# Mean squares from the input rows and convolution taps on sixteen 32 by 32 tiles, in a streaming encoder step

## The chip, the core and the metric

The kernel runs on one core of a Trainium2 chip. The metric is the device time of one execution in microseconds. The kernel before was run three times: 1377.0, 1381.54 and 1380.49 us, median 1380.49.

## The reference, cut to what matters

Two layers over 544 tokens (512 prompt frames and 32 frames of a running stream) with 1024 channels. Layer 0 is attention beside a gated linear recurrence, layer 1 a convolution module; each is followed by a squared-ReLU MLP. The change touches the first normalisation and the depthwise convolution:

```python
def rms_norm(x, g):
    xf = x.astype(jnp.float32)
    y = xf * lax.rsqrt(jnp.mean(xf * xf, axis=-1, keepdims=True) + EPS)
    return (y * g.astype(jnp.float32)).astype(x.dtype)

def conv_module(xn, buf, w1, b1, w_dw, b_dw, ln_g, ln_b, w2, b2):
    u = xn @ w1 + b1
    u = u[..., :D_MODEL] * jax.nn.sigmoid(u[..., D_MODEL:])
    full = jnp.concatenate([buf.astype(u.dtype), u], axis=1)
    y = lax.conv_general_dilated(full, w_dw.astype(full.dtype)[:, None, :], window_strides=(1,),
                                 padding='VALID', dimension_numbers=('NWC', 'WIO', 'NWC'),
                                 feature_group_count=D_MODEL) + b_dw
    y = jax.nn.silu(layer_norm(y, ln_g, ln_b))
    return y @ w2 + b2, full[:, -(CONV_W - 1):]
```

The depthwise convolution has 31 taps per channel (`CONV_W` = 31), and it is causal: the prompt is preceded by 30 zeros, the running stream by 30 cached rows.

## The kernel before

**Layout.** Activations lie with channels on the 128 partitions and tokens along the free dimension: `resid` is 8 channel tiles (`KT`) of 544 tokens. Each projection streams weights in units of 256 output columns (two halves m of 128). SP loads a unit to `w_raw`, ACT copies it to `w_h` as fp32r (`split_hi`, L585), DVE subtracts to get `w_l` (`split_lo`, L1456), and TensorE (PE) sums three products, w_h by x_h, w_h by x_l and w_l by x_h, each in two column halves of 272: 96 fp32r matmuls per unit (L983, or L1006 where both halves m advance together). Two double-bank slots of PSUM hold the two halves m. Semaphores order everything: `w_lo` counts split units, `gemm_done` finished halves, `slot_free` evacuated slots, `xl_ready` finished input tiles.

**Prologue.** SP loads the input rows (`x_rows`, L365, L366), then weight unit 0, then 19 small parameter transfers (L368 to L385), then weight unit 1. PE transposes the rows into channel tiles through the two slots (L944). DVE copies each tile to `resid` (L1511); ACT multiplies by the norm's gain into `x_h` (L615) and squares the tile (L606); POOL adds the squares (L460); DVE makes `x_l` (L1478). The split of unit 0 stands within these loops: at k = 3 on ACT, at k = 5 on DVE. PE transposes the parameters before unit 0 (L947 to L957) and takes the mean of the squares by a matmul with `mean_d` between the two halves of unit 0 (`mean_square`, L1041, L968). ACT takes the root (L621), DVE the reciprocal over 544 columns (L1484), and the result `r_tok` scales every evacuation of the first projection (L1548).

**Convolution stage.** Unit m of the first pointwise projection gives the two halves of channel tile m. ACT takes the sigmoid (L853); DVE makes the gated frames `glu` (`gated_frames`, L1849). The 31 taps of a tile are split: PE does 14 (16 in the last tile, m = 7) and DVE 17 (15). On PE a tap is a matmul with a diagonal matrix. The array is used as four tiles of 64 by 64: the diagonal is `fold` (two halves of the identity added) scaled by the tap's weights (ACT, L862), a tap t takes `glu` straight, its partner t + 7 takes `glu_swap`, a copy with the two halves of the partitions exchanged that POOL's queue makes by two transfers per tile (L557). `add_taps` (L1353) issues, for each of 7 pairs and 2 column halves of 288, four matmuls in plain fp32, 56 per tile; each fp32 matmul appears as two MATMUL records in the trace, 112 per tile. The columns cover prompt, gap and running stream in one row of 576 (`CW`). DVE runs its 17 taps over the same 576 columns on two accumulators (`conv_taps`, L1871, L1875, L1878) with the next unit's `split_lo` after the eighth, then adds the four PSUM parts in two instructions and the two accumulators in one (`conv_sum`, L1888, L1890). PE's order is: `gated(m+1)`, then the taps of m, and so on; after the last, matmuls with `mean_d` (L1363) take the channel mean for LayerNorm, with the taps of tile 7 after the third of them. `keep_clock` (L959) issues bf16 matmuls into an unused bank, only to keep PE active.

The lines that set the order around the change:

```python
            pairs = tap_pairs(m)
            pe.wait_ge(conv_ready, m + 1)
            x = glu[:, m, :]
            for pair in pairs:
                for c in range(2):
                    for across in range(2):
                        for r in range(2):
```

Of the kernel before, what the change touches and what calls it, by code (L numbers as in the profile page):

```python
# [41 lines left out]
PE_TAPS = 14  # L42
PAIRS = PE_TAPS // 2
LAST_PAIR = (PE_TAPS, PE_TAPS + 1)
CROSS = LAST_PAIR[1] + 1 - PAIRS
# [39 lines left out]
def hybrid_kernel(nc, x_prompt, x_sample, cache_a_k, cache_a_v, state_b, cache_c, norm_mix_g, norm_ffn_g,  # L85
# [35 lines left out]
    dw_swap = sb(ctx, "dw_swap", [P, KT, CROSS])  # L121
# [9 lines left out]
    no_use = sb(ctx, "no_use", [P, 1])  # L131

# [15 lines left out]
    with ExitStack() as over:  # L148
        sb(over, "under_x", [P, 2, KT, TOK])
        with ExitStack() as mix:  # L150
            x_rows = sb(mix, "x_rows", [P, TT + 1, D])
            dw_rows = sb(mix, "dw_rows", [CONV, D])
            dw_cross = sb(mix, "dw_cross", [CROSS, D])
            cc_rows = sb(mix, "cc_rows", [PAD, D])

# [20 lines left out]
        with ExitStack() as mix:  # L176
# [6 lines left out]
            glu_swap = sb(mix, "glu_swap", [P, 2, FW])  # L183
            diag = sb(mix, "diag", [P, 2, PE_TAPS + 2, P // 2])
            fold = sb(mix, "fold", [P, P // 2])
# [45 lines left out]
    def width(c):  # L231
# [8 lines left out]
    consts = sem("consts")  # L240
    gains_T, gains_ready = sem("gains_T"), sem("gains_ready")
    r_ready = sem("r_ready")
# [31 lines left out]
    glu_edges, conv_step, conv_ready, cvmean, cv_centred, cv_sq, cv_var, cv_std, cv_norm, cv_silu = (  # L274
        sem(n) for n in ("glu_edges", "conv_step", "conv_ready", "cvmean", "cv_centred", "cv_sq",
                         "cv_var", "cv_std", "cv_norm", "cv_silu"))
    cv_hi, cv_lo, swapped = sem("cv_hi"), sem("cv_lo"), [sem("swapped0"), sem("swapped1")]
# [58 lines left out]
    def tap_pairs(m):  # L336

        return [(t, t + PAIRS) for t in range(PAIRS)] + ([LAST_PAIR] if isinstance(m, int) and m == KT - 1 else [])

# [22 lines left out]
    def _(sp):  # L362
# [5 lines left out]
        def load_parameters():  # L368
# [9 lines left out]
            for h in range(2):  # L378
                to, of = (a.rearrange("t (k h c) -> t k h c", h=2, c=P // 2) for a in (
                    dw_cross[:], c_w_dw[0, PAIRS:PAIRS + CROSS]))  # L380
                sp.dma_start(to[:, :, h, :], of[:, :, 1 - h, :]).then_inc(rows_landed, 16)
# [49 lines left out]
    def _(pool):  # L431
# [8 lines left out]
        pool.memset(ones[:], 1.0)  # L440
        pool.memset(mean_d[:], 1.0 / D)
        pool.memset(eps[:], EPS)
# [27 lines left out]
        for k in range(KT):  # L470
            sum_squares(0, k, k % 2, k == 0)

# [12 lines left out]

        pool.wait_ge(xl_ready, KT)
# [62 lines left out]
        pool.tensor_tensor(fold[:], ident[:, 0:P // 2], ident[:, P // 2:P], ALU.add).then_inc(glu_edges, 1)  # L549

        for m in range(KT):
# [3 lines left out]
            for b in range(2):  # L555
                to, of = slice(b * (P // 2), (b + 1) * (P // 2)), slice((1 - b) * (P // 2), (2 - b) * (P // 2))
                pool.dma_start(glu_swap[to, m % 2, :], glu[of, m, :]).then_inc(swapped[m % 2], 16)  # L557
# [9 lines left out]
    def _(act):  # L567
# [33 lines left out]
        def square(n, k, parity, ready, at):  # L601

            act.wait_ge(ready, at)
            if not (n == 0 and isinstance(k, int) and k < 2):
                act.wait_ge(sumsq_step, k + (8 * n - 1))
# [17 lines left out]
        act.wait_ge(consts, 1)  # L623
# [7 lines left out]
        act.wait_ge(vec_ready, 1)  # L631
        act.activation(wlr_h[:, :, 0:RANK], wlr[:], ACT.Copy).then_inc(wlr_hi, 1)
# [34 lines left out]
        for u in range(U_ATT):  # L667
# [4 lines left out]
            if u == 0:  # L672
                frame_std(0)
# [3 lines left out]
            if u < 4:  # L677
                square_qk(u, 0)
                square_qk(u, 1)
        copy_rows(6)  # L680
# [175 lines left out]
        def diagonals(i, s):  # L856
# [3 lines left out]
            for pair in tap_pairs(m):  # L860
                for t, w, at in ((pair[0], w_dw, m * CONV + pair[0]), (pair[1], dw_swap, m * CROSS + (pair[1] - PAIRS))):
                    ins = act.activation(diag[:, s, t, :], fold[:], ACT.Identity,  # L862
# [1136 lines left out]
```

## Time and profile before

| | |
|---|---|
| median of the three runs | 1380.49 us |
| time of the profiled execution | 1379.77 us |
| its span, first to last instruction | 1378.0 us |
| PE, DVE, ACT, POOL busy | 1348.9, 722.5, 466.7, 82.1 us |
| convolution stage: `gated(1)` to the last mean matmul | 767.7 to 918.6 us of the span |

Busy shares are averages over stages with different limits; for a change in one stage, the chain of waits and the timeline of that stage are the views to read. Matmuls are pipelined: the duration of one record includes filling and draining, and the distance between starts is what it costs.

### The profile page before, as it was taken

How to read it: one execution, taken by the hardware profiler on the slowest of the kernel's cores; microseconds unless marked ns; L12 is line 12 of the kernel's file. 1: busy time of each engine (PE TensorE's matmuls, PEld its weight loads, DVE VectorE, ACT ScalarE, POOL GpSimd, SP SyncE). 2: the span in 40 equal slices, each digit the busy share in tenths (PEclk: the TensorE clock that was granted, in tenths of full speed). 3: DMA queues.
4: the chain of work that ended last, by engine and by line, in shares of the span. 5: the costliest groups of instructions: out<-in, count | busy, mean ns of one | idle time of the engine just before them, and what ended most of it. 6: DMA issues, size and time to landing. Idle time of an engine off the chain costs nothing.

```text
span 1378.0 us, 26679 instructions
## 1 busy us (share of the span) xinstructions
PE 1348.9 (98%) x11208; PEld 1279.1 (93%) x11208; DVE 722.5 (52%) x1034; ACT 466.7 (34%) x743; POOL 82.1 (6%) x116
## 2 busy tenths in 40 slices
PE   6999999999999999999999999999999999999998
PEld 5999788789999999999999888868999999999998
DVE  6684568675543334334324799897544333324322
ACT  4221556534333213223122433336333213213121
POOL 5100100001100000000011000001100000000000
PEclk9999999999999999999999999999999999999999
DMA  5422410122222222222221222112222322222221
GB/s 172 158 76 86 150 32 1 70 97 85 69 92 92 92 92 92 92 74 79 96 88 62 75 77 80 52 39 69 93 92 79 97 77 85 92 92 92 92 78 49
DMA packets 105590, 115.62 MB, mean 84 GB/s; under 512 B 3761, under 2 KB 102684, under 8 KB 105245
## 3 DMA queue, kind: packets, MB, share of 16 engines
q1 hardware_dynamic: 102621, 101.47, 22.9%
q0 software_dynamic: 2816, 12.84, 2.9%
q8 instruction: 69, 1.13, 0.3%
q14 instruction: 20, 0.16, 0.0%
q10 hardware_dynamic: 64, 0.02, 0.0%
HBM read 104.62 MB, written 7.21 MB: 81 GB/s over the span
## 4 chain that ended last, share of the span: by engine, by line
PE 90%; DVE 5%; ACT 3%; issue 1%; DMA 0%; POOL 0%; SPq 0%; ACTq 0%; DVEq 0%; POOLq 0%
PE ps L983 70%; PE ps L1353 4%; PE ps L1116 4%; PE ps L1006 2%; DVE rstd L1552 2%; PE ps L1133 1%; PE ps L964 1%; PE ps L1227 1%; PE ps L1166 1%; PE ps L1150 1%; PE ps L1022 1%; DVE w_l L1456 1%; PE ps L968 1%; ACT w_h L585 1%; PE ps L1363 1%
## 5 line engine op out<-in xcount | busy, mean ns | idle before, releaser
L585 ACT ACTIVATE w_h<-w_raw 128x2048 fp32r<-128x2048 f32 x92 | 175.3, 1905 | 274.0 <-PE ps L983 270.9
L1456 DVE TENSOR_TENSOR w_l<-w_raw,w_h 128x2048 fp32r<-128x2048 f32 x92 | 211.7, 2301 | 104.5 <-ACT w_h L585 104.4
L983 PE MATMUL ps<-x_h,w_h 128*128 128x272 f32 x1184 | 247.6, 291 | 2.6 <-ACT sig L853 1.5
L983 PE MATMUL ps<-x_l,w_h 128*128 128x272 f32 x1184 | 245.6, 289 | 0.0
L983 PE MATMUL ps<-x_h,w_l 128*128 128x272 f32 x1184 | 245.3, 289 | 0.0
L983 PE MATMUL ps<-xf_l,w_h 128*128 128x272 f32 x1024 | 211.0, 288 | 0.0
L983 PE MATMUL ps<-xf_h,w_h 128*128 128x272 f32 x1024 | 211.0, 288 | 0.0
L983 PE MATMUL ps<-xf_h,w_l 128*128 128x272 f32 x1024 | 210.5, 287 | 0.0
L983 PEld LDWEIGHTS ps<-x_h,w_h 128*128 128x128 f32 x1184 | 187.2, 190 | 6.8 <-issue 6.3
L983 PEld LDWEIGHTS ps<-x_h,w_l 128*128 128x128 f32 x1184 | 187.4, 190 | 0.0
L983 PEld LDWEIGHTS ps<-x_l,w_h 128*128 128x128 f32 x1184 | 186.5, 189 | 0.0
L983 PEld LDWEIGHTS ps<-xf_h,w_l 128*128 128x128 f32 x1024 | 160.7, 188 | 0.0
L983 PEld LDWEIGHTS ps<-xf_h,w_h 128*128 128x128 f32 x1024 | 160.4, 188 | 0.2
L983 PEld LDWEIGHTS ps<-xf_l,w_h 128*128 128x128 f32 x1024 | 160.1, 188 | 0.0
L1796 DVE TENSOR_TENSOR resid<-ps,resid 128x544 f32 x64 | 46.3, 723 | 198.2 <-PE ps L983 197.2
L829 ACT ACTIVATE relu<-relu 128x544 f32<-128x544 f32 x64 | 42.2, 659 | 237.7 <-DVE relu L1814 237.7
L983 PE MATMUL ps<-odd_h,w_h 128*128 128x272 f32 x512 | 106.0, 288 | 0.0
L983 PE MATMUL ps<-odd_l,w_h 128*128 128x272 f32 x512 | 105.6, 288 | 0.0
L983 PE MATMUL ps<-odd_h,w_l 128*128 128x272 f32 x512 | 105.4, 287 | 0.0
L1814 DVE SCALAR_TENSOR_TENSOR relu<-ps,xn 128x544 f32<-128x544 f32 x64 | 46.2, 722 | 87.4 <-PE ps L983 87.3
L983 PEld LDWEIGHTS ps<-odd_h,w_l 128*128 128x128 f32 x512 | 80.3, 188 | 0.0
L983 PEld LDWEIGHTS ps<-odd_h,w_h 128*128 128x128 f32 x512 | 80.1, 189 | 0.1
(258 smaller groups left out, 1682.6 us busy)
## 6 DMA issues: line engine op xcount, KB each, us to landing
w_raw<-in_w_ffn_up SPq DMA_DIRECT2D x32, 1024.0 KB, 5.4
w_raw<-in_w_ffn_down SPq DMA_DIRECT2D x32, 1024.0 KB, 5.1
w_raw<-in_w_in_ab SPq DMA_DIRECT2D x12, 1024.0 KB, 5.2
w_raw<-in_c_w_pw SPq DMA_DIRECT2D x12, 1024.0 KB, 5.8
w_raw<-in_w_out_ab SPq DMA_DIRECT2D x4, 1024.0 KB, 5.3
glu_swap<-glu POOLq DMA_DIRECT2D x16, 151.5 KB, 2.5
resid_scratch<-resid POOLq DMA_DIRECT2D x1, 2176.0 KB, 7.5
resid<-resid_scratch POOLq DMA_DIRECT2D x1, 2176.0 KB, 8.9
```

Of the source, the lines that this page charges most:

```text
L585: act.activation(w_h[s][:], w_raw[:, s], ACT.Copy).then_inc(w_hi, 1)
L829: act.activation(relu2[:, m, :], relu[:, m, :], ACT.Square).then_inc(relu2_done, 1)
L964: pe.matmul(ps[:, bank, 0:2 * P], any_bits[:, 0:P], any_bits, start=True, stop=True)
L968: ins = pe.matmul(dst[:, a, :], w[:], src[:, a * n:(a + 1) * n], start=start, stop=stop)
L983: ins = pe.matmul(ps[:, 2 * m + t, 0:HALF], a[s][:, k, w], b[:, k, t * HALF:(t + 1) * HALF], start=(k == 0 and q == 0), stop=(k == KT - 1 ...
L1006: ins = pe.matmul(ps[:, 2 * m + t, 0:HALF], a[s][:, k, w], b[:, k, t * HALF:(t + 1) * HALF], start=(k == 0 and q == 0), stop=(k == KT - 1 ...
L1116: ins = pe.matmul(ps[:, 2 * m + t, 0:HALF], a[u % 2][:, k, m * P:(m + 1) * P], b[:, k, t * HALF:(t + 1) * HALF], start=(k == 0 and q == 0) ...
L1353: ins = pe.matmul(sum_ps(r, CH)[to, c, :], diag[rows, s, tap, :], src, start=(pair is pairs[0]), stop=(pair is pairs[-1]))
L1456: dve.tensor_tensor(w_l[s][:], w_raw[:, s], w_h[s][:].bitcast(F32), ALU.subtract).then_inc(w_lo, 1)
L1552: dve.reciprocal(rstd[:, 0:TOK], sumsq[:]).then_inc(rstd_ready, 1)
L1796: dve.tensor_tensor(r, slot(m), r, ALU.add).then_inc(slot_free[m], 1)
L1814: dve.scalar_tensor_tensor(out=halves(relu[:, m, :]), in0=slot(m), scalar=0.0, in1=halves(r_tok), op0=ALU.max, op1=ALU.mult).then_inc(slot ...
```

## The change

**Prologue.** The mean squares come from the input rows, where tokens are partitions: DVE squares and sums rows 0 to 2 (`tensor_tensor_reduce`), ACT rows 3 and 4 (`Square` with `accum_out`), then root and reciprocal run on a 128 by 5 tile, POOL widens it (`r_wide`), and PE transposes it within unit 0 into the slot that is not in use. The transposes of x use four slots of two banks; ACT copies tiles 6 and 7 in place of DVE. DVE does all its copies first, then the split of unit 0, then the `x_l`. Unit 0 runs both halves m together. The parameters are loaded after both first weight units (23 transfers in place of 19) and transposed after unit 0. PE issues 16 bf16 matmuls at the start and 24 between the first transposes.

**Convolution.** `ROTS` = 4, `SET` = 6: tap j*6 + n takes a copy of `glu` rotated by 32*j partitions; 5 rounds n (6 in tile 7) of 4 rotations and 4 row groups: 80 matmuls of 512 columns on 32 by 32 tiles per channel tile (96 in the last). DVE has 11 taps (7 in the last) over 512 columns; the running stream's 32 frames are computed by DVE as one product over all windows and one reduction. Six transfers per tile instead of two, 20 diagonals (24) of 32 columns instead of 14, four PSUM additions instead of two. On DVE the sum of tile m-1 now comes after the gated frames of m, and the split after the taps.

```diff
-PE_TAPS = 14
+ROTS = 4
+SET = 6
+PE_TAPS = ROTS * SET
@@ SP
             if first:
                 for s in range(2):
                     sp.dma_start(w_raw[:, s], source(s)).then_inc(w_landed[s], 16)
-                    if s == 0:
-                        load_parameters()
+                load_parameters()
@@ POOL
-        for k in range(KT):
-            sum_squares(0, k, k % 2, k == 0)
...
+        pool.wait_ge(r_rows, 1)
+        pool.tensor_copy(r_wide[:], x_rs[:].unsqueeze(2).to_broadcast((P, TT + 1, P))).then_inc(r_spread, 1)
...
+            for j in range(1, ROTS):
+                at = P - j * (P // ROTS)
+                pool.dma_start(glu_rot[0:at, m % 2, j - 1, :], glu[P - at:P, m, 0:PAD + SEQ]).then_inc(moved[m % 2], 16)
+                pool.dma_start(glu_rot[at:P, m % 2, j - 1, :], glu[0:P - at, m, 0:PAD + SEQ]).then_inc(moved[m % 2], 16)
@@ ACT
+        act.activation(no_use[:], eps[:], ACT.Sqrt)
         act.wait_ge(gains_ready, 1)
         for k in range(KT):
-            hi_gain(0, x_h, k, V_MIX, slot_free[k % 2], k // 2 + 1)
-            if k == 3:
+            hi_gain(0, x_h, k, V_MIX, x_copied[k % 4], k // 4 + 1)
+            if k == 1:
                 split_hi(0, 0, 0)
-            square(0, k, k % 2, slot_free[k % 2], k // 2 + 1)
+                for late in (6, 7):
+                    act.wait_ge(gemm_done, late + 1)
+                    act.activation(resid[:, late, :], flat(late % 4)[:, 0:TOK], ACT.Copy).then_inc(x_copied[late % 4], 1)
...
+        act.activation(x_rs[:], x_ss[:], ACT.Sqrt, bias=eps[:, 0:1], scale=1.0 / D).then_inc(std_ready, 1)
@@ PE
+        pe.wait_ge(ones_ready, 1)
+        keep_clock(16, 6)
...
+                    keep_clock((0, 14, 6, 2, 2)[c], 6)
...
+        def x_ready(k):
+            if k == KT - 2:
+                pe.wait_ge(r_spread, 1)
+                for c in range(TT + 1):
+                    M = width(c)
+                    ins = pe.transpose(flat(2)[:, c * P:c * P + M], r_wide[0:M, c, :], ident[0:M, 0:M])
+                ins.then_inc(r_T, 1)
+            pe.wait_ge(xl_ready, X_MIX0 + k + 1)
...
+        together(0, 0, x_h, x_l, x_ready)
+        parameters()
...
+        def taps(m):
+            s = m % 2
+            pe.wait_ge(diag_ready, m + 1)
+            pe.wait_ge(slot_free[1], m + (tile0(U_PW1) // 2 + 1))
+            pe.wait_ge(moved[s], (m // 2 + 1) * 96)
+            if m:
+                pe.wait_ge(conv_step, m * STEPS)
+            for n in range(rounds(m)):
+                for j in range(ROTS):
+                    for r in range(ROTS):
+                        rows, to = (slice(h * (P // ROTS), (h + 1) * (P // ROTS)) for h in (r, (r + j) % ROTS))
+                        tap = j * SET + n
+                        src = glu_rot[rows, s, j - 1, tap:tap + SEQ] if j else glu[rows, m, tap:tap + SEQ]
+                        ins = pe.matmul(ps[to, 4 + r, :], diag[rows, s, tap, :], src, start=(n == 0),
+                                        stop=(n == rounds(m) - 1))
+            ins.then_inc(taps_done, 1)
...
+        for m in range(1, KT):
+            gated(m)
+            taps(m - 1)
         pe.wait_ge(slot_free[0], tile0(U_PW2) // 2)
-        for k in range(3):
+        for k in range(4):
             add_mean(k)
-        add_taps(KT // 2 - 1, 1)
+        taps(KT - 1)
@@ DVE
+        for c in range(3):
+            dve.wait_ge(x_landed[c], 16)
+            if c:
+                dve.wait_ge(x_sums, c)
+            dve.tensor_tensor_reduce(sq[:].rearrange("p a t -> p (a t)")[:, 0:D], x_rows[:, c, :], x_rows[:, c, :], 1.0,
+                                     0.0, ALU.mult, ALU.add, x_ss[:, c:c + 1]).then_inc(x_sums, 1)
...
+        for k in range(KT - 2):
+            dve.wait_ge(gemm_done, k + 1)
+            dve.tensor_copy(resid[:, k, :], flat(k % 4)[:, 0:TOK]).then_inc(x_copied[k % 4], 1)
+        split_lo(0, 0, 0)
+        for k in range(KT):
+            dve.wait_ge(x_copied[k % 4], k // 4 + 1)
+            lo_gain(k, X_MIX0, x_l, x_h, V_MIX)
...
+        def conv_sample(i, d):
+            m = i * 2 + d
+            u = at(glu, m)
+            row = u[:, SAMPLE:SAMPLE + DEC]
+            win = bass.AP(tensor=row.tensor, offset=row.offset, ap=[list(row.ap[0]), [1, DEC], [1, CONV]],
+                          runtime_checks=row.runtime_checks)
+            tap = at(w_dw, m).unsqueeze(1).to_broadcast((P, DEC, CONV))
+            y = at(cv, m)[:, SAMPLE:SAMPLE + DEC]
+            dve.tensor_tensor(windows[:], win, tap, ALU.mult).then_inc(conv_window, 1)
+            dve.wait_ge(conv_window, 3 * m + 1)
+            dve.tensor_reduce(y, windows[:], mybir.AxisListType.X, ALU.add).then_inc(conv_window, 1)
...
+            for n in range(first, first + ROTS):
+                to = (y, odd)[n % 2]
+                dve.wait_ge(conv_step, m * STEPS + (n - 1))
+                dve.tensor_tensor(to, ps[:, 4 + n - first, :], to, ALU.add).then_inc(conv_step, 1)
...
         with dve.Fori(0, KT // 2 - 1) as i:
-            for s in range(2):
-                gated_frames(i, s)
-                conv_taps(i, s)
-                conv_sum(i, s)
+            for d in range(1, 3):
+                gated_frames(i, d)
+                conv_sum(i, d - 1, NT)
+                conv_taps(i, d, dve_taps(0))
+                conv_sample(i, d)
+                split_lo(U_PW1, i, d + 2)
```

## Rows read from the trace of the kernel before

**Rows 1.** The page: busy time by engine, and shares of the chain that ended last

```profile
PE 1348.9 (98%) x11208; PEld 1279.1 (93%) x11208; DVE 722.5 (52%) x1034; ACT 466.7 (34%) x743; POOL 82.1 (6%) x116
...
PE 90%; DVE 5%; ACT 3%; issue 1%; DMA 0%; POOL 0%; SPq 0%; ACTq 0%; DVEq 0%; POOLq 0%
```

**Rows 2.** The chain in order of time, convolution stage: start us, us, what

```profile
767.72 12.29 PE ps L983 x96
780.01 6.97 PE ps L1353 x112
...
895.34 6.96 PE ps L1353 x112
902.30 3.11 PE ps L1363 x12
905.41 7.93 PE ps L1353 x128
913.35 5.25 PE ps L1363 x20
918.60 0.87 PE ps L964 x8
```

**Rows 3.** The chain in order of time, prologue

```profile
35.80 3.56 DVE xn L1484
...
40.25 12.25 PE ps L983 x96
```

**Rows 4.** Timeline of the prologue: start us, us, engine line op, out<-in, xcount

```profile
9.90 0.72 DVE L1511 COPY resid<-ps 128x544 f32<-128x544 f32 x1 [3.40 <-PE ps L944]
...
14.37 2.68 PE L944 MATMUL ps<-ident,x_rows 128*128 128x128 f32 x10 [0.72 <-DVE resid L1511]
...
24.86 0.82 PE L983 MATMUL ps<-x_h,w_h 128*128 128x272 f32 x2
...
25.48 0.66 PE L983 MATMUL ps<-x_l,w_h 128*128 128x272 f32 x2
...
25.93 0.65 PE L983 MATMUL ps<-x_h,w_l 128*128 128x272 f32 x2
...
32.97 1.08 PE L968 MATMUL ps<-sumsq,mean_d 128*128 128x272 f32 x4
```

**Rows 5.** Timeline, PE, two stretches with small matmuls

```profile
128.53 1.03 PE L1062 MATMUL ps<-ident,proj 128*128 128x128 f32 x8
...
273.23 0.36 PE L1227 MATMUL ps<-lev 64*32 64x16 f32 x12
```

**Rows 6.** Timeline, DVE, from the sum of channel tile 0 into the taps of tile 1

```profile
787.13 0.76 DVE L1888 TENSOR_TENSOR cv<-ps,cv 128x576 f32 x1 [3.56 <-PE ps L1353]
...
788.59 0.76 DVE L1890 TENSOR_TENSOR cv<-cv,rstd 128x576 f32 x1
789.26 1.03 DVE L1849 SCALAR_TENSOR_TENSOR glu<-ps,vecs,sig 128x272 f32 x3
790.69 0.58 DVE L1871 TENSOR_SCALAR cv<-glu,w_dw,vecs  x1 [0.40 <-DVE glu L1849]
...
791.61 0.81 DVE L1878 SCALAR_TENSOR_TENSOR cv<-glu,w_dw,cv  x1
792.34 0.81 DVE L1878 SCALAR_TENSOR_TENSOR rstd<-glu,w_dw,rstd 128x576 f32<-128x576 f32 x1
...
795.99 2.29 DVE L1456 TENSOR_TENSOR w_l<-w_raw,w_h 128x2048 fp32r<-128x2048 f32 x1
```

**Rows 7.** Groups by line, shapes apart: DVE at 288 columns, ACT's diagonals

```profile
L1910 DVE SCALAR_TENSOR_TENSOR cv<-ps,cv 128x288 f32<-128x288 f32 x16 | 5.9, 447 | 0.8 <-PE ps L1363 0.8
...
L862 ACT ACTIVATE diag<-fold,w_dw 128x64 f32<-128x64 f32 x57 | 19.0, 333 | 1.7 <-PE ps L1353 1.7
```

**Rows 8.** Timeline, POOL: the two transfers of channel tile 1; then their time to landing

```profile
790.59 1.30 POOL L557 DMA_DIRECT2D glu_swap<-glu  x2 [19.95 <-DVE glu L1849]
...
DMA to landing us min/median/max: 2.4/2.5/3.3
```

More of the change, by code:

```diff
@@ L334, in hybrid_kernel, with rounds, pe_taps, dve_taps @@
     CH = CW // 2
-    def tap_pairs(m):
-        return [(t, t + PAIRS) for t in range(PAIRS)] + ([LAST_PAIR] if isinstance(m, int) and m == KT - 1 else [])
+    def rounds(m):
+        return SET if isinstance(m, int) and m == KT - 1 else SET - 1
+    def pe_taps(m):
+        return [j * SET + n for n in range(rounds(m)) for j in range(ROTS)]
+    def dve_taps(m):
+        return [t for t in range(CONV) if t not in pe_taps(m)]
+    STEPS = CONV - ROTS * (SET - 1) + ROTS
+    SAMPLE = SEQ + PAD
     def cv_half(c):
@@ L679, in _ @@
                 square_qk(u, 1)
+            if u == 0:
+                act.wait_ge(vec_ready, 1)
+                act.activation(wlr_h[:, :, 0:RANK], wlr[:], ACT.Copy).then_inc(wlr_hi, 1)
         copy_rows(6)
@@ L1088, in gates @@
                 mean_of(sum_ps(n), lr, gate_w[:, n * P:(n + 1) * P]).then_inc(gate_done, 1)
-        x_ready = lambda k: pe.wait_ge(xl_ready, X_MIX0 + k + 1)
-        unit(0, 0, 0, x_h, x_l, x_ready, mean_square)
+        def x_ready(k):
+            if k == KT - 2:
+                pe.wait_ge(r_spread, 1)
+                for c in range(TT + 1):
+                    M = width(c)
+                    ins = pe.transpose(flat(2)[:, c * P:c * P + M], r_wide[0:M, c, :], ident[0:M, 0:M])
+                ins.then_inc(r_T, 1)
+            pe.wait_ge(xl_ready, X_MIX0 + k + 1)
+        for n in range(4):
+            pe.wait_ge(x_copied[n], 2)
+        together(0, 0, x_h, x_l, x_ready)
+        parameters()
         for u in range(1, U_ATT - 1):
+            if u == 2:
+                pe.wait_ge(vec_ready, 1)
+                pe.wait_ge(r_ready, 1)
             if 2 <= u < 6:
@@ L1448, in _ @@
         dve.engine_nop().then_inc(taps_done, 2)
+        dve.engine_nop().then_inc(sumsq_step, KT)
+        dve.engine_nop().then_inc(sq_ready, KT)
+        dve.engine_nop().then_inc(ms_ready, 1)
+        for m in range(2):
+            dve.engine_nop().then_inc(slot_free[m], KT // 2)
         dve.wait_ge(gains_T, 1)
@@ new lines, in parameters @@
+        def parameters():
+            dve.wait_ge(vec_T, 2)
+            own(dve.tensor_copy(vecs[:, V_B1:V_N], ps[:, 7, V_B1:V_N]))
+            for k in range(4):
+                dve.tensor_scalar(g_qk[:, k:k + 1], vecs[:, V_QG:V_QG + 1], DA ** -0.5, None, ALU.mult)
+                dve.tensor_copy(g_qk[:, 4 + k:5 + k], vecs[:, V_KG:V_KG + 1])
+            dve.tensor_copy(w_dw[:].rearrange("p k c -> p (k c)"), ps[:, 7, V_N:V_N + KT * CONV])
+            dve.tensor_copy(dw_rot[:].rearrange("p k c -> p (k c)"), ps[:, 7, V_N + KT * CONV:V_N + KT * (CONV + CROSS)])
+            dve.wait_ge(vec_T, 3)
+            dve.tensor_copy(cc_T[:].rearrange("p k c -> p (k c)"), ps[:, 6, 0:KT * PAD]).then_inc(vec_ready, 1)
+            near = 384 + NREL - 1
+            dve.tensor_copy(rel_u[:, 0, 0:383], rel[:, NREL - 1:NREL].to_broadcast((HA, 383))).then_inc(rel_built, 1)
+            dve.tensor_copy(rel_u[:, 0, 383:near], rel[:, ::-1]).then_inc(rel_built, 1)
+            dve.tensor_copy(rel_u[:, 0, near:640], rel[:, 0:1].to_broadcast((HA, 640 - near))).then_inc(rel_built, 1)
@@ L1590, in _ @@
                     gate_minima()
+            if u == 0:
+                parameters()
+            if u == 1:
+                low_rank_weights()
         copy_rows(G_CK + 1)
```

260 lines of the change are left out of this document (113 added, 147 removed).

## The prediction

> **What bounds the kernel now.** I read the page first: PE is busy 98% of the span and makes 90% of the chain that ended last [rows 1]. So work on another engine pays only where PE waits for it. Then I read the chain in order of time for the two stretches that the change touches. In the convolution stage it is PE without a break: 12.29 us of projection, 6.97 us of taps, and so on, seven tap blocks of 6.97 and a last one of 7.93, with matmuls for the mean around it, to 918.60 [rows 2]. What shortens PE there shortens the kernel, until DVE takes over. In the prologue the chain runs through DVE: the reciprocal for the frame scale takes 3.56 us from 35.80, then an evacuation, and the second projection unit starts at 40.25 [rows 3]. Before it PE does nothing but wait and transpose until its first product at 24.86 [rows 4].
>
> **The sum is made** against the profiled execution, 1379.77 us, 0.7 below the median of 1380.49. A difference under 0.3% (4 us) I count as no change.
>
> **Part 1, prologue.** The x rows arrive unchanged; DVE copied the first tile at 9.90 [rows 4]. New ahead of it are 24 keep-active matmuls. Eight of them took 0.87 us at the fast clock, 0.109 each [rows 2]; at the slow level twice that. They fill waits for rows that are being loaded, but at the slow clock (24 x 0.218 = 5.2 us from about 6.5) they overrun them: the first tile is ready at 9.8 to 12.5, I take 11. DVE's three row sums lie before that, since the rows land while PE still transposes. Then DVE does six copies of 0.72 (to 15.3), the split of 2.3 [rows 6] (17.6) and the first x_l: PE starts at 18.4 in place of 24.86. For this the transposes must keep up with DVE's 0.72 per tile. At the fast clock eight transposes took 1.03 us, fill included, so five cost about 0.55 [rows 5]. At the slow one ten took 2.68, so 1.3 per tile [rows 4]: the start would then be about 22.4. ACT's part (two x_h, split, two copies, six x_h, each about as long as a copy) ends near 21, its two row squares and the root near 23; DVE waits about 1 us for the root at its sixth x_l, and PE wants the scale only at k = 6, near 27.5: hidden.
>
> Unit 0 lasted from 24.86 to 40.25, 15.4 us: 12.25 of matmuls [rows 3], about 1.0 for the mean [rows 4] and 2.1 more, because PE had done little before: its first pairs start 0.45 apart [rows 4], not the 0.256 of 12.25/96, so it ran at 1.2 and not 2.4 GHz. After: 12.25, 0.6 for five transposes of the scale, 2.7 for 25 parameter transposes at 0.109, which cover DVE's two evacuations: 15.5. Unit 1 starts at 33.9, 6.3 us earlier. **Prologue: -6.3**, bounds -0.5 (slow transposes and a slow start; a loss has no place, as nothing is added ahead of the first product that is longer than what went) and -9 (first tile at 9.8, parameters at half price). Costed at nothing: the 19 parameter loads, now 23 and behind weight unit 1, since SP has until 31 us for them; the 25 small transposes' readers on DVE (under 2 us), covered by unit 1's 12.25; POOL's widening, which has 4 us. Behind it, the query and key units are paced by ACT and DVE as much as by PE, but they all move with unit 1.
>
> **Part 2, taps on PE.** Before: 112 records in 6.97 us, 62.2 ns apart. Four tiles work at once, for one record of this shape on the full array costs 5.25/20 = 262 ns (the mean matmuls, same 288 columns) [rows 2], four times 62 and a little. So a tile needs 249 ns per record of 288 columns, 0.864 ns per column. After: 160 records of 512 columns, 442 ns each on their tile. With all sixteen tiles at work that is 27.6 ns per record, 4.42 us; filling and emptying sixteen tiles once more adds one record, 0.4. **I take 4.8 us per tile.** No row shows sixteen tiles, so bounds: above, no closer starts than now, 160 x 62.2 = 9.95 us; below, 4.4. I stay near the lower end because twelve small matmuls of 32 columns came in 0.36 us with their drain [rows 5], under 30 ns each, so PE can start them so fast, at least in a burst. The last block has 192 records: 5.8 against 7.93.
>
> **DVE beside it.** Prices by distances of starts [rows 6]: gated frames 1.0; a tap at 576 columns 0.73, at 512 0.67 (1.08 ns per column, from 758 ns at 576 and 447 at 288 columns [rows 6, 7]); the first two taps 0.9. Eleven taps: 0.9 + 9 x 0.67 = 6.9. Four PSUM additions at 0.6 and one final one: 3.2 with its wait. The running stream: two passes over 992 elements, 1.13 each, a small one and two waits: 2.5. Split 2.2. Sum **15.8 us** per channel tile, against 12.29 + 4.8 = **17.1** on PE. DVE idles a little while it waits for the taps (after its gated frames), and catches up: PE stays the bound, with about 1 us to spare. Before, DVE had 3.56 us idle [rows 6] in a period of 19.25. ACT needs 20 diagonals at 0.24 (a 333 ns row overlaps its neighbours), 4.8 us [rows 7]: under the 12.29. POOL: two transfers took 1.30 us, so six about 3.5, and 2.5 to 3.3 to land [rows 8]; the taps of m come 12 us after its frames, hidden. Only in the last tile are they near: the frames of tile 7 are ready 3 us after its unit, so the copies land at +9.3, while PE has the taps of tile 6 and four means until +8.95: 0.4 us of wait.
>
> **Sum of part 2.** Six steady periods: 6 x (6.97 - 4.8) = 13.0. The end, from the last unit's end at 895.34 to 918.60, is 23.3 now; after: 9.3 + 5.8, then DVE's sum of tile 7 (3.2) beside three means, one mean (1.05): 19.4. Saved 3.9. **Convolution: -16.9.** The normalisation behind is not touched.
>
> **Total:** 1379.8 - 6.3 - 16.9 = 1356.6 us.
>
> **Rivals.**
> A, forecast: both parts work, PE stays the bound. 1350 to 1361. Chance 0.56.
> B, DVE becomes the bound in the convolution. The windowed product reads overlapping windows and a repeated tap row, and every PSUM addition waits on the one before the last; 2.2 us more per tile makes 18.0, so six periods save 7.5 and the end about 3: 1363. For it: only 1.3 us lie between the two engines. Against it: prices per element were the same for all shapes here. Chance 0.16. The Trainium skill says under "TensorEngine Tiling (Array Packing)", PSUM Bottleneck, that evacuation can become the limit once tiling speeds up the matmuls; no row shows it yet, as DVE's own 3.56 us of waiting at the sum [rows 6] is for PE.
> C, the prologue gives little: the clock stays at 1.2 GHz through the transposes, PE starts at 22.4 and slow. 1362. Chance 0.13.
> D, other side: starts of tap matmuls come no closer than now. Place: the tap block on PE. Price: 9.95 us per block and 11.9 in the last, 7 x 2.98 + 4.0 = 24.9 more; total 1379.8 - 6.3 + 24.9 = 1398. It decides from about 48 ns per record: 1312 x 0.0484 = 63.5 us is what the blocks take now (56.7) plus the prologue's 6.8. With half the tiles at work at once (55 ns) the sum is 1388. For it: over the tap blocks the trace never shows less than 62 ns. Against it: 62 is just what four tiles explain, and the burst above. Chance 0.13, both prices together.
> The Trainium skill, "TensorE: Matmul & The Clock Gate", Back-to-back issue gap, names about 62 ns per matmul as the limit of one way of decoding, which would give case D; its section on packing small matmuls reports 10.6 times for sixteen tiles, which speaks for A. The burst agrees with the second, but it is short.
> E, no net change: a partial D eats the prologue's gain. 0.02.
>
> **Numbers.** Faster by over 0.3%: A, B, C, 0.85, less a doubt for what I have not seen: 0.82. Within 0.3%: 0.04. Slower: 0.14. The range takes in A, B and C and their bounds: 1349 to 1374; left out are D and what little lies below.
>
> **What would show it.** Right: the chain in the convolution stays PE, with blocks of 160 records in 4.4 to 5.0 us and a period of 17; the first product at 17 to 20 us, unit 1 at 32 to 35, L1484's reciprocal gone from the first projection. Wrong for the taps: blocks over 5.5 us. B: pieces of DVE in the chain between tap blocks, PE waiting for gated frames or for w_lo. C: transposes 0.21 us apart and first pairs 0.45 apart.

## The result and the profile after

The changed kernel takes 1371.67 us (median of 7, 1370.97 to 1374.85), the kernel before 1378.99 in the same session (7 runs, 1375.78 to 1381.54): ratio 0.9947, 95% interval 0.9935 to 0.9958. It is faster, by 7.3 us where 23.2 were forecast. The profiled execution took 1374.85 us, its span 1373.1. It is the slowest of the seven, 3.2 us above their median, so what its trace shows of the clock need not hold for the others.

The chain of waits of after in the first 45 us. Columns here and in every chain: start in us, duration in us, what.

```profile
10.40 4.06 PE ps L996 x26
17.32 0.79 DVE x_l L1536
18.25 10.83 PE ps L1040 x72
...
34.58 10.51 PE ps L1017 x82
```

The first product starts at 18.25 in place of 24.86, and unit 1 at 34.58 in place of 40.25 [rows 3, 4]: 5.7 us gained. L1484's reciprocal is no longer in the chain.

The same view for the convolution stage; it answers to [rows 2].

```profile
765.27 12.30 PE ps L1017 x96
777.58 5.45 PE ps L1398 x151
783.03 12.26 PE ps L1017 x96
...
866.14 5.47 PE ps L1398 x148
...
890.51 6.70 DMA glu_rot<-glu
...
897.45 8.87 PE ps L1398 x186
...
909.61 1.24 PE ps L1414 x4
910.85 0.87 PE ps L980 x8
```

Three things are to be seen. A tap block takes 5.45 us, not 4.8. The last tile's copies land so late that PE, which was done with the tap block and the means before it at 893.4, stands for 4.1 us until 897.45. And the last block then takes 8.87 us. From the start of the stage (`gated(1)`, 765.27) to the end of the means (910.85) it is 145.6 us, before 150.9 [rows 2]: 5.3 saved of the 16.9 forecast.

The stage also starts too late. It started at 767.72 before and now at 765.27, 2.4 us earlier, though unit 1 was 5.7 us earlier. And after the stage's end, 7.75 us earlier (918.60 to 910.85), the span ends only 4.9 us earlier (1378.0 to 1373.1). So 3.2 us went between the prologue and the convolution and 2.9 behind it, in stages that the diff does not touch. The starts of ACT's weight split (one per unit, paced by PE) show where. Each pair of rows spans 31 units of the first MLP, then 27 of the second; before:

```profile
360.26 1.90 ACT L585 ACTIVATE w_h<-w_raw 128x2048 fp32r<-128x2048 f32 x1
732.51 1.90 ACT L585 ACTIVATE w_h<-w_raw 128x2048 fp32r<-128x2048 f32 x1
...
1012.63 1.90 ACT L585 ACTIVATE w_h<-w_raw 128x2048 fp32r<-128x2048 f32 x1
1340.92 1.90 ACT L585 ACTIVATE w_h<-w_raw 128x2048 fp32r<-128x2048 f32 x1
```

and after:

```profile
355.92 1.90 ACT L608 ACTIVATE w_h<-w_raw 128x2048 fp32r<-128x2048 f32 x1
729.85 1.90 ACT L608 ACTIVATE w_h<-w_raw 128x2048 fp32r<-128x2048 f32 x1
...
1004.88 1.90 ACT L608 ACTIVATE w_h<-w_raw 128x2048 fp32r<-128x2048 f32 x1
1336.08 1.90 ACT L608 ACTIVATE w_h<-w_raw 128x2048 fp32r<-128x2048 f32 x1
```

The first stretch takes 373.93 us where it took 372.25, the second 331.20 where it took 328.29: 12.062 and 12.267 us per unit against 12.008 and 12.159. These are the same 96 matmuls of 272 columns per unit, with the same operands, on a PE that is never idle. Over 32 units each that is 1.7 and 3.5 us.

Most of the rest of the 3.2 us is clock. The windows view of after, PE alone (columns: stretch, length, busy us with count, granted clock as a share of 2.4 GHz, DMA share, GB/s):

```profile
138.00:144.00 6.00, 6.00 (x23) 0.50 0.80 273
...
896.00:902.00 6.00, 4.55 (x82) 0.50 0.01 3
903.00:911.00 8.00, 7.80 (x120) 1.00 0.01 2
```

At 138 us PE ran at 1.2 GHz, from 137.9 to 144.7; before, it did so for half as long (145.3 to 148.7). The same view over the whole stretch, before and then after:

```profile
135.00:155.00 20.00, 17.37 (x118) 0.91 0.55 185
...
135.00:155.00 20.00, 17.95 (x106) 0.83 0.51 174
```

Across it the lead over the kernel before falls from 5.4 us (122.68 against 117.27 in the two chains) to 3.75 (154.18 against 150.43), 1.7 us. Some 0.6 us come back before the first MLP, where the kernel before has a slow stretch (298.9 to 302.3) that after lacks, and the MLP takes its 1.7: that makes the 3.2, with a few tenths in the other projection units. The 1.2 GHz level also stands over the last tap block (895.7 to 902.5). It begins while PE idles for its 4.1 us.

### The profile page after: what moved, and what is told of

It reads as the page before. It is cut to its first block, busy times and chain, and to the rows that moved or that the text cites. A ratio compares the mean times of both kernels' runs of the same rounds, so it can differ in the third digit from the quotient of the medians.

```text
span 1373.1 us, 27650 instructions
## 1 busy us (share of the span) xinstructions
PE 1344.9 (98%) x11649; PEld 1274.7 (93%) x11649; DVE 703.2 (51%) x1028; ACT 472.7 (34%) x792; POOL 86.5 (6%) x145
## 4 chain that ended last, share of the span: by engine, by line
PE 90%; DVE 5%; ACT 2%; issue 2%; DMA 1%; POOL 0%; SPq 0%; DVEq 0%; ACTq 0%; POOLq 0%
PE ps L1017 70%; PE ps L1173 4%; PE ps L1398 3%; PE ps L1040 3%; DVE rstd L1613 2%; PE ps L1190 1%; PE ps L1284 1%; PE ps L980 1%; PE ps L1223 1%; PE ps L1207 1%; PE ps L1056 1%; PE ps L1002 1%; DVE w_l L1514 1%; PE ps L1438 1%; DMA x_rows<-in_x_sample 1%
## 5 line engine op out<-in xcount | busy, mean ns | idle before, releaser
L1017 PE MATMUL ps<-x_h,w_h 128*128 128x272 f32 x1152 | 242.0, 292 | 2.4 <-ACT sig L894 1.5
L1017 PE MATMUL ps<-x_l,w_h 128*128 128x272 f32 x1152 | 238.6, 288 | 0.0
L1017 PE MATMUL ps<-x_h,w_l 128*128 128x272 f32 x1152 | 238.2, 288 | 0.0
L1017 PEld LDWEIGHTS ps<-x_h,w_h 128*128 128x128 f32 x1152 | 180.9, 189 | 9.1 <-issue 8.7
L1017 PEld LDWEIGHTS ps<-x_l,w_h 128*128 128x128 f32 x1152 | 182.6, 189 | 0.0
L1017 PEld LDWEIGHTS ps<-x_h,w_l 128*128 128x128 f32 x1152 | 180.7, 188 | 0.0
L1017 PEld LDWEIGHTS ps<-odd_l,w_h 128*128 128x128 f32 x512 | 80.8, 188 | 0.0
```

Of the source, the lines that this page charges most:

```text
L1017: ins = pe.matmul(ps[:, 2 * m + t, 0:HALF], a[s][:, k, w], b[:, k, t * HALF:(t + 1) * HALF], start=(k == 0 and q == 0), stop=(k == KT - 1 ...
```

## The experiments

Four questions: does each part bring its share alone (e1, e2); what does the end of the convolution cost and why (e3, e4, e11); why do untouched matmuls slow down (e5, e6, e9, e10); what sets 34 ns per tap record (e7). e8 puts the repairs together. Each kernel was timed against the kernel before on the same chip (its medians 1379.92, 1380.93 and 1379.46 us in the three sessions: e1 to e4, e5 to e8, e9 to e11). So two runs of different sessions are compared by their ratios; 0.001 is 1.4 us.

| run | median us | ratio to before, 95% interval | chain: stage start, end of means |
|---|---|---|---|
| after | 1371.67 | 0.9947 (0.9935 to 0.9958) | 765.27, 910.85 |
| e1 prologue only | 1377.26 | 0.9985 (0.9974 to 0.9996) | 765.21, 915.90 |
| e2 convolution only | 1372.7 | 0.9942 (0.9929 to 0.9956) | 767.99, 913.93 |
| e3 tail clock | 1371.73 | 0.9939 (0.9926 to 0.9952) | 764.09, 906.92 |
| e4 frames first | 1367.63 | 0.9912 (0.9899 to 0.9925) | 761.77, 900.93 |
| e5 before, moved | 1382.45 | 1.0013 (1.0004 to 1.0023) | |
| e6 after, place kept | 1363.22 | 0.9875 (0.986 to 0.989) | 765.08, 910.08 |
| e7 two per tile | 1396.49 | 1.0116 (1.0101 to 1.0131) | 765.14, 933.26 |
| e8 frames, place | 1358.5 | 0.9846 (0.9833 to 0.986) | 759.35, 897.75 |
| e9 e8, 32 bytes on | 1365.02 | 0.9906 (0.9878 to 0.9935) | |
| e10 e8, 160 bytes on | 1365.92 | 0.9909 (0.9886 to 0.9932) | |
| e11 weights held | 1369.99 | 0.9928 (0.9908 to 0.9948) | 769.39, 909.64 |

### e1 and e2: one part alone

e1 is the change without its convolution: taps, transfers, diagonals and DVE's part are those of before, and the parameter loads are 19 again. e2 is its complement.

```diff
@@ e1, against after (constants, taps, transfers, diagonals and DVE's tap code as before)
-PE_TAPS = ROTS * SET
+PE_TAPS = 14
...
-            glu_rot = sb(mix, "glu_rot", [P, 2, ROTS - 1, PAD + SEQ])
+            glu_swap = sb(mix, "glu_swap", [P, 2, FW])
...
@@ e2, against after (row sums, root, widening, transposes and loads of the prologue as before)
-    x_ss = sb(ctx, "x_ss", [P, TT + 1])
-    x_rs = sb(ctx, "x_rs", [P, TT + 1])
...
```

> The kernel before with the new prologue alone. Theory: the two parts add up. The second projection unit starts at 34.6 us as in the changed kernel (40.25 before), and of the 5.6 us most arrives at the end: 1373 to 1375, against 1379 before; the convolution keeps its period of 19.2 us. Rival: later stages absorb the early start (the attention, where the changed kernel's lead fell from 5.4 to 3.7 us): 1377 or more.

> The kernel before with the new convolution alone. Theory: six periods of 17.7 in place of 19.2 us give 9, the end of the stage gives back 3.7 (27 us from the last unit's end to the last mean, 23.3 before): 1373 to 1375. Rival: the convolution is worth what the prediction said, about 17, and the prologue costs time elsewhere: 1363.

e1 gains 0.15% (2 us), less than the 4 to 6 us of its theory; its 1377.26 is the time of its rival. e2 gains 0.58% (8 us), at 1372.7 just past its theory's 1373 to 1375 and far from its rival's 1363. In e1 the taps are those of before, as the chain shows, and everything from there on is PE without a break:

```profile
777.48 6.96 PE ps L1392 x112
...
902.72 7.93 PE ps L1392 x128
```

e1's lead is small from the start, in this execution at least: its transposes took 6.23 us at half clock, where after's took 4.06, and unit 1 started at 37.44, 2.8 us ahead of before (40.25). It still has 2.5 us at the convolution and 2.7 behind it (915.90 against 918.60), but only 0.8 at the end of the span (1377.2 against 1378.0). e1's MLP units take 12.036 and 12.239 us: slower than before as well, but not as slow as after. e2's take 11.956 and 12.159, so e2 gets 1.6 us in the first MLP that its edit does not touch. The sum of the two parts alone is 10 us, more than the 7.3 of both, but with some 1.6 us of uncertainty on each of the three the difference is hardly clear of noise. e2 shows the slow last block too, again behind a wait for the copies:

```profile
892.55 7.56 DMA glu_rot<-glu
900.35 9.05 PE ps L1359 x187
```

### e3: PE kept active before the last tap block

```diff
         for k in range(4):
             add_mean(k)
+        pe.wait_ge(slot_free[1], tile0(U_PW2) // 2)
+        keep_clock(32, 2)
         taps(KT - 1)
```

> The changed kernel with 32 keep-active matmuls (3.5 us) before the taps of channel tile 7, where PE stood idle for 4.1 us waiting for the rotated copies. Theory: the wait stays, but the clock does not fall to half (0.5 from 895.7 to 902.5 us in the changed kernel), so the last tap block takes 6.5 in place of 8.9 us: 2 to 3 us faster than 1371.7, 1369. Rival: the last block is long because it has 192 records and DVE beside it, not for the clock: no change.

```profile
892.37 3.49 PE ps L980 x32
895.87 6.53 PE ps L1398 x179
905.68 1.24 PE ps L1414 x4
```

Here 32 small matmuls fill the wait, PE stays at 2.4 GHz and the last block of 192 records takes 6.53 us, 34.0 ns each, in place of 8.87. So 2.3 us of the long last block were the clock. From stage start to end of means it is 142.8 us, 2.8 under after. The time does not decide it: the ratio is 0.9939 where after has 0.9947, 1.1 us less, and the intervals overlap and leave room for 2.3 us as well as for none. What is shown is the profiled execution's 2.3 us; how many other executions of after have them stays open.

### e4: the last tile's frames first

DVE computed the running stream's taps of tile 6 and split a weight unit ahead of the gated frames of tile 7, and these frames are what the copies wait for. e4 peels the last turn of the loop and moves the frames ahead.

```diff
+        def after_frames(i, d, last=False):
+            conv_sum(i, d - 1, NT)
+            conv_taps(i, d, dve_taps(0))
+            if last:
+                gated_frames(KT // 2 - 1, 1)
+            conv_sample(i, d)
+            split_lo(U_PW1, i, d + 2)
...
-        gated_frames(KT // 2 - 1, 1)
```

> The changed kernel with DVE's gated frames of tile 7 moved ahead of the running stream's product of tile 6 and of the split, so that the rotated copies start 2 us earlier and before the weight transfer that the split releases. Theory: the copies were late because they started late and shared the DMA engines with 1 MB of weights; now they land in 3.2 us after the last issue, before PE asks for them, the wait of 4.1 us and the slow clock behind it go: 6 us faster, 1365 to 1367. Rival: the landing of 5 to 6.7 us is the price of six transfers themselves, without weights beside them: the wait shrinks by 2 us only, 1369 to 1370.

```profile
885.80 4.08 PE ps L1414 x16
889.87 6.53 PE ps L1398 x175
```

The last block follows the means with no wait, at full clock. From stage start to end of means: 139.2 us, 6.4 under after. The ratio falls from 0.9947 to 0.9912, 4.8 us (4.0 between the medians), where 6 were expected. The DMA view of this kernel from 870 to 890 us (columns: count, KB each, median us to landing):

```profile
glu_rot<-glu POOLq DMA_DIRECT2D x2, 203.2 KB, 2.8
...
```

### e11: the weights held back

In after the same six copies land slowly. DMA view, 880 to 900 us:

```profile
w_raw<-in_c_w_pw SPq DMA_DIRECT2D x1, 1024.0 KB, 6.4
glu_rot<-glu POOLq DMA_DIRECT2D x2, 203.2 KB, 5.9
...
```

A weight unit of 1 MB was issued at 886.91, just ahead of the copies (887.98 to 890.51). It is so in every tile of after but the first: the change put DVE's split, which releases the next weights, right ahead of the next frames, so that the copies of tile 2, say, start at 799.46, behind weights at 798.39. In the kernel before the copies started at 790.59 and the next weights at 798.45, 7.9 us behind them. In the steady tiles the slow landing costs nothing: the copies of tile 2 are wanted at 813.0.

The unit of 886.91 is split by ACT only at 943.7. e11 has the unit before it, which after issues at 869.24, wait for the last tile's copies. The one of 886.91 stands behind it in SP's order, so both come later, at 898.50 and 899.40. That costs nothing behind the stage: from its end to the end of the span it is 462.3 us (909.64 to 1371.9), as in after.

```diff
                     sp.wait_ge(w_lo, i * 2 + (u0 + s - 1))
+                    if hold and s:
+                        sp.wait_ge(moved[1], KT // 2 * 96)
                     sp.dma_start(w_raw[:, s], source(i * 2 + s)).then_inc(w_landed[s], 16)
...
-        stream(U_PW2, 4, columns(c_w_pw2[0]))
+        stream(U_PW2, 4, columns(c_w_pw2[0]), hold=True)
```

> The changed kernel with the 1 MB weight transfer of the second output unit held back until the last channel tile's six copies have landed; the transfer is not needed until that unit, some 20 us later. After has the last copy landing 6.4 to 6.7 us behind its issue and PE idle 4.1 us before the last tap block. Theory, the weights share the DMA engines with the copies: the copies land 2.5 to 4 us behind the issue, at 893.5 to 895 instead of 897.2, PE's wait is 0.5 to 2 us and the kernel 2 to 4 us under after's 1371.7. Rival, the six copies are slow by themselves (they do not land sooner): 6.4 us, a wait of 4.1 us and 1371.7 us within 1 us.

Lines of its chain, and then of its DMA view from 880 to 900 us:

```profile
894.62 3.66 DMA glu_rot<-glu
...
898.52 6.59 PE ps L1400 x182
```

```profile
glu_rot<-glu POOLq DMA_DIRECT2D x2, 203.2 KB, 3.1
...
```

The copies come 3.66 us behind their last issue in place of 6.70, in the range expected. PE waits about 1 us (the last unit ends at 769.39 + 118.6, the block and the means take 9.6 more, the last block starts at 898.52), and that block runs at full clock. So the copies were slow because of what shared the DMA engines. The stage takes 140.25 us in place of 145.6. By the ratios the time lies 2.6 us under after's (1.7 between the medians); this ratio's interval (0.9908 to 0.9948) holds after's 0.9947, so the time alone does not show it. (Its stage starts late, at 769.39, because this profile, as e1's and e6's, has the prologue's transposes at half clock. Its execution, like e6's, was the slowest of its runs: 1373.64 us, and 1370.42 for e6.)

### e5, e6, e9, e10: the place of the activations in memory

The change allocates `x_ss` and `x_rs` (a place of 32 bytes per partition each) and a `dw_rot` that is 288 bytes larger than `dw_swap`, all ahead of `x_h`. So `x_h`, `x_l` and every activation tensor behind them moved: by 64 bytes in e1, 288 in e2, 352 in after. e5 moves them by 64 in the kernel before and changes nothing else; e6 puts the two small tensors elsewhere in the changed kernel.

```diff
     no_use = sb(ctx, "no_use", [P, 1])
+    sb(ctx, "pad", [P, 16])                      (e5, on the kernel before)
...
-    x_ss = sb(ctx, "x_ss", [P, TT + 1])          (e6, on after)
-    x_rs = sb(ctx, "x_rs", [P, TT + 1])
...
             r_wide = sb(mix, "r_wide", [P, TT + 1, P])
+            x_ss = sb(mix, "x_ss", [P, TT + 1])
+            x_rs = sb(mix, "x_rs", [P, TT + 1])
```

> The kernel before with one unused tensor of 64 bytes per partition behind no_use, so that x_h and every activation tensor behind it lie 64 bytes further on, as they do in e1_prologue_only; no instruction is added. In the two MLP stages the average unit took 12.01 and 12.16 us before and 12.04 and 12.24 in e1_prologue_only. Theory, the place of the activations in memory sets the pace of the 272-column matmuls: 12.04 and 12.24 us here too, and the kernel slower than before by about 3 us (31 units x 0.03 + 31 x 0.08). Rival, the place or count of the instructions does it (the prologue's edit changes what lies ahead of the unit loops in PE's program): 12.01 and 12.16, and the time of before within 1 us.

> The changed kernel with the two small tensors x_ss and x_rs put behind r_wide, in memory that only the prologue uses, so that x_h and what follows lie where e2_conv_only has them; the instructions are those of after. Theory, place in memory: MLP units of 11.96 and 12.16 us, as e2_conv_only, against 12.06 and 12.27 of after, which is 3.3 us in the first and 3.3 us in the second MLP: 1365 to 1367 us where after has 1371.7. Rival, the instructions: units stay at 12.06 and 12.27 and the time at 1371.7 within 1 us.

The same splits around 31 units of the first MLP; e5, and then e6:

```profile
360.78 1.90 ACT L586 ACTIVATE w_h<-w_raw 128x2048 fp32r<-128x2048 f32 x1
733.89 1.90 ACT L586 ACTIVATE w_h<-w_raw 128x2048 fp32r<-128x2048 f32 x1
```

```profile
359.25 1.90 ACT L608 ACTIVATE w_h<-w_raw 128x2048 fp32r<-128x2048 f32 x1
729.87 1.90 ACT L608 ACTIVATE w_h<-w_raw 128x2048 fp32r<-128x2048 f32 x1
```

e5: 373.11 / 31 = 12.036 us, and in the second MLP (1013.84 to 1344.30) 330.46 / 27 = 12.239, e1's numbers per unit to the nanosecond, with no instruction changed. The kernel is 0.13% slower, 1.8 us (0.6 to 3.2) where about 3 were expected. e6: 370.62 / 31 = 11.956, and (1003.56 to 1331.85) 328.29 / 27 = 12.159, e2's numbers. The place of the tensors is the cause, and the rival (the count or place of the instructions) falls: each pair has the same unit times with different instructions.

e6's time falls by 9.9 us against after by the ratios (0.9875 and 0.9947; 8.4 between the medians), more than the 3.3 and 3.3 that I reckoned for the MLPs, to below the range expected. The other units share the gain: in the convolution stage the 96 matmuls take 12.16 us in place of 12.26, and over the whole kernel there are 92 units; 0.106 us on each would make 9.8. e4 and e8, which differ in the place alone, are 9.1 us apart.

e9 and e10 move e8's tensors on by 32 and 160 bytes.

> e8_frames_place with one unused tensor of 32 bytes per partition behind no_use: x_h and what follows lie 32 bytes further on, at an address with the same remainder by 256 as in e1_prologue_only and e5_before_moved. Theory A, only the place within 256 bytes counts: MLP units of 12.04 and 12.24 us, as in those two, against 11.96 and 12.16 of e8, and a kernel slower than e8's 1358.5 by about 5 us. Theory B, the place within a longer stretch counts: a pair of durations not seen so far. Rival, the place does nothing and e5 and e6 agreed with it by chance: 11.96 and 12.16, 1358.5 us within 1 us.

> e8_frames_place with x_h and what follows 160 bytes further on, which is the first multiple of 512. No theory says which place is best; the four seen gave 11.96 to 12.06 and 12.16 to 12.27 us per unit. If a round address serves PE best, units come out under 11.96 and 12.16 and the kernel under 1358.5 us; if only what shares the memory with it counts, it lands somewhere within the four and the kernel between 1357.5 and 1366 us.

Both give 12.04 and 12.24 us per unit (e9 12.035, 12.239; e10 12.036, 12.239) and 1365.0 and 1365.9 us. So e9's theory A holds, though with 128 bytes in place of 256, since e10's address has another remainder by 256. A round address is not the best one. All kernels fall into four classes by the remainder of `x_h`'s address by 128:

| remainder by 128 | kernels (address of `x_h`) | first MLP, us per unit | second |
|---|---|---|---|
| 0 | e1, e5 (111232), e9 (111488), e10 (111616) | 12.035 to 12.036 | 12.239 |
| 32 | after, e3, e4, e7, e11 (111520) | 12.062 | 12.267 |
| 64 | before (111168) | 12.008 | 12.159 |
| 96 | e2, e6, e8 (111456) | 11.956 | 12.159 |

That the remainder by 128 is what counts is read from remainder 0 alone, where three addresses agree; the other rows have one address each. Why PE's operand stream depends on it stays open, and so does whether it is the operand's own place or its place against the weights or against what DVE and ACT write meanwhile.

### e7: two rounds per tile, one behind the other

In after, the 34 ns per record are not even. The timeline of a block's start (columns: start, time to the last end of the group, engine, line, operation, tiles, shape, count):

```profile
777.51 0.63 PE L1398 MATMUL ps<-glu,diag 32*32 32x512 f32 x4
777.53 0.69 PE L1398 MATMUL ps<-glu_rot,diag 32*32 32x512 f32 x12
777.96 0.61 PE L1398 MATMUL ps<-glu,diag 32*32 32x512 f32 x4
777.99 0.66 PE L1398 MATMUL ps<-glu_rot,diag 32*32 32x512 f32 x12
778.39 0.84 PE L1398 MATMUL ps<-glu,diag 32*32 32x512 f32 x4
778.63 0.79 PE L1398 MATMUL ps<-glu_rot,diag 32*32 32x512 f32 x12
```

Sixteen records start together, sixteen more 0.45 us behind, as the prediction had it (442 ns per record and tile). Then there is a gap: one record starts at 778.39, the others of its sixteen only from 778.58 on, and 32 records take 1.07 us from there on instead of 0.88. It looks as if PE held some 32 matmul records (16 fp32 matmuls, one round over the sixteen tiles) and took in more only as the first ones end, 0.6 us after their start. e7 has the same matmuls in another order. It puts four records of a tile behind each other, so that 32 records in a row go to eight tiles:

```diff
-            for n in range(rounds(m)):
-                for j in range(ROTS):
-                    for r in range(ROTS):
+            for n0 in range(0, rounds(m), 2):
+                for j, r, n in [(j, r, n) for j in range(ROTS) for r in range(ROTS)
+                                for n in range(n0, min(n0 + 2, rounds(m)))]:
```

> The changed kernel with the tap matmuls in another order: two rounds of a tile one behind the other before the next tile gets its own, so that 64 records in a row go to eight tiles only instead of to sixteen; same matmuls, same loads. After has 34 ns per record (5.45 us per block). Theory, PE holds only some 32 outstanding load and matmul pairs and each leaves the queue when it is complete: with twice as many behind each other on a tile, fewer tiles are at work in that window, 50 to 59 ns per record, blocks of 8 to 9.5 us and a kernel slower than after by 18 to 28 us. Rival, 34 ns is the rate at which PE starts such matmuls whatever tile they go to: 5.45 us blocks, 1371.7 us within 1 us.

The expectation's "64 records in a row go to eight tiles only" is twice too many for this edit; it is 32 records that go to eight tiles. Its price stands: 442 ns shared by eight is 55 ns, within its 50 to 59.

```profile
777.38 0.65 PE L1398 MATMUL ps<-glu,diag 32*32 32x512 f32 x4
777.43 0.65 PE L1398 MATMUL ps<-glu_rot,diag 32*32 32x512 f32 x4
777.83 0.63 PE L1398 MATMUL ps<-glu,diag 32*32 32x512 f32 x4
```

and in its chain:

```profile
777.45 8.82 PE ps L1398 x160
```

Now only eight records start together (nine in later groups), and the block takes 8.82 us, 55 ns per record, as that theory expected. The kernel takes 1396.5 us, by the ratios 23.3 more than after. A fixed rate of starts would have left the block at 5.45. The number of tiles that a short stretch of the instruction order touches sets the rate; that this stretch is a window of 32 records is read from the two orders and not varied. The Trainium skill, "TensorE: Matmul & The Clock Gate", "Architectural detail: the array is 16× 32×32, not 1× 128×128", gives TensorE's queue a depth of 64, in which weight loads can be pulled ahead of matmuls. 32 matmul records with their loads would be 64 entries, so the trace agrees with the depth, but no run here varied it. It shows more reordering than that: in e7 the first records of eight tiles start within 0.09 us, ahead of three more records of the first tile that stand before them in the program.

### e8: both repairs

e4's order with e6's places.

```diff
+            if last:
+                gated_frames(KT // 2 - 1, 1)
...
-    x_ss = sb(ctx, "x_ss", [P, TT + 1])
+            x_ss = sb(mix, "x_ss", [P, TT + 1])
```

> e4_frames_first (the last channel tile's gated frames ahead of the sample taps of the tile before, so that the last taps find their copies landed) with x_ss and x_rs put as in e6_after_place_kept. Theory, place in memory: the 6 us of e6 come off the 1367.6 of e4_frames_first as well, 1361 to 1363 us, faster than before and than after. Rival, the instructions set the pace in the MLPs: 1367.6 us within 1 us.

```profile
759.35 12.18 PE ps L1017 x96
771.53 5.45 PE ps L1398 x150
...
886.70 6.52 PE ps L1398 x181
...
897.75 0.87 PE ps L980 x8
```

1358.5 us, a little better than the 1361 to 1363 expected, faster than before by 1.5% and than after by 1.0%. This is the version to keep: the same two parts as the change, with one step of DVE's order moved and two tensors of 20 bytes put elsewhere.

## Why the prediction was wrong

The direction was right and the time lies in the range, but the gain was a third of the forecast. In the profiled execution 1374.85 - 1356.6 = 18.2 us are missing (15.1 in the median), and each row of this table is read from the chains above. That the time lies in the range is luck: the range was drawn for slow transposes and for a slow DVE, and in the profiled execution the time was lost elsewhere.

| step | forecast | measured | missing |
|---|---|---|---|
| unit 1 starts earlier | 6.3 | 5.7 | 0.6 |
| from there to the convolution ("they all move with unit 1") | 0 | -3.2 | 3.2 |
| six steady periods | 13.0 | 9.0 | 4.0 |
| last unit's end to the end of the means | 3.9 | -3.7 | 7.6 |
| behind ("is not touched") | 0 | -2.9 | 2.9 |

**Prologue: right.** First product 18.25 (18.4 forecast), unit 0 and what lies in it to 34.58 (33.9); it took 16.3 us and not 15.5. It is a matter of the execution, though: in e1's profile the 26 transposes took 6.23 us at half clock (4.06 in after), the first product started at 20.71 and unit 1 at 37.44. Rival C's slow transposes are what some executions do: those of the profiles of e1, e6 and e11.

**Taps on PE: the mechanism right, a term mis-sized.** The step is "filling and emptying sixteen tiles once more adds one record, 0.4": a wait of some 0.2 us comes not once but at every round (1.07 us for 32 records and not 0.88), 5.45 us per block and not 4.8 (0.65 x 6 = 3.9 us). The burst of twelve small matmuls that kept me at the lower end could not tell: its row has tiles of 64 by 32 and 16 moving columns, not sixteen tiles and 512. Rival D's rate did not come: 34 ns is well under 62. The Trainium skill, "TensorE: Matmul & The Clock Gate", Back-to-back issue gap, has about 62 ns per matmul for one way of decoding, which would be an estimated 9.9 us per block; the trace does not agree. Case D's other price, half the tiles, is what e7 shows. Two figures of case D were off without changing it: the prologue's gain is 6.8 there and 6.3 in the sum, and 55 ns per record makes 1389, not 1388.

**DVE beside it: right.** No piece of DVE stands between steady tap blocks; B did not happen.

**The end: wrong, the largest miss.** The step is "the copies land at +9.3, while PE has the taps of tile 6 and four means until +8.95: 0.4 us of wait". The last unit ended at 883.9, the frames were ready at +3.8 (+3 forecast), the last copy was issued at +6.6, and the copies landed at +13.3. The 2.5 to 3.3 us to land came from transfers that had the DMA engines to themselves; here a megabyte of weights lay ahead (e11: 3.66 in place of 6.70), and of a wait of 0.4 I did not ask what grows with it. It became 4.1 us, and behind it PE ran most of the last block at 1.2 GHz: 8.87 us and not 5.8, of which 2.3 are the clock (e3) and 0.7 the mis-sized rate of the taps. e4 took away the wait, by earlier frames and by copies that no longer share their time with the weights. DVE's work was counted, but its order was not used: the sample taps and a split stand ahead of frames on which the last block depends.

**The untouched stages: wrong.** "They all move with unit 1" and "is not touched" hold for instructions. They do not hold for places in memory: the change moved every activation tensor by 352 bytes, which cost 1.7 us in the first MLP and 3.5 in the second. e6 gets back 9.9 us over the whole kernel, more than was lost, since its place is better than that of the kernel before. About 1.7 us more are clock in the attention stage, where the slow stretch has two lengths or is missing, from profile to profile.

## What to carry to other kernels

When an edit adds a tensor, look at what the allocator moves: in a kernel that is bound by PE, compare the distances of identical matmuls in stages that the edit does not touch, and try a few places before judging the edit. Where many small tiles share the array, order the matmuls round by round, so that every tile comes once before any comes again. A wait near zero ahead of the last block is not a small term: price the copy with the transfers that share its time, and add the slow clock that a few us of idle PE may bring.

## What the runs showed of the hardware

- Same instructions, same data, PE never idle: 96 matmuls of 128x272 take 11.956 to 12.062 us in the first MLP and 12.159 to 12.267 in the second, by the place of the activations alone, repeated to about a nanosecond in every kernel with the same remainder by 128.
- Sixteen 32 by 32 tiles with 512 fp32 columns take 34 ns per record (after); with eight at work it is 55 (e7).
- Six copies of 0.81 MB together land in 2.6 to 3.7 us alone (e4, e11) and in 5.2 to 6.7 behind a 1 MB transfer (after).
- Behind the prologue PE ran at 1.2 GHz in stretches of 3.4 or 6.8 us. One lies over the last tap block where PE had idled 3.9 to 5.0 us before it (after, e2, e6), and none where it idled 1.0 us (e11), 0.3 (e7) or not at all (e3, e4, e8). One lies around 140 us in the attention stage, in every profile but e4's. Others lie around 299 us (before, e6, e11) and some 20 us behind the convolution stage (all but e1, e3, e4 and e11).
